# The first feed-forward layer of a fused two-block kernel as seven half-wide products in place of eight

## The chip, the cores and the metric

The kernel runs on one core of one Trainium2 chip, as one program. The metric is device time in microseconds (us) from launch to end. All data of the case is float32. The engines are called PE (TensorE), ACT (ScalarE), DVE (VectorE), POOL (GpSimd) and SP (SyncE, which only issues transfers here).

## What is computed

Two transformer-like blocks follow each other on 1024 tokens of width 1024. The change touches the feed-forward part of the first block:

```
h = rms_norm(x, g_pre_mlp[i])
f = jnp.square(jax.nn.relu(h @ w_up[i])) @ w_down[i]
x = x + rms_norm(f, g_post_mlp[i])
```

`w_up` is 1024 x 4096 and `w_down` 4096 x 1024. What is ahead of it (attention, convolution, a gated mix and the projection `w_o`) and what is behind it (a gate, and the whole second block) computes the same before and after the change.

## The kernel before, in words

Everything lies transposed: features on the 128 partitions, tokens along a row. The 1024 tokens are done in two halves of 512 (`HALF`), called `h` 0 and 1. A float32 product is made of three passes in a shorter float type: each operand is split into a high part (a cast on ACT) and a low part (the rest, a subtraction on DVE), and PE adds high x high, high x low and low x high (`three_passes`). One output tile of 128 features x 512 tokens over 1024 input features is thus 8 x 3 = 24 matmuls of 512 columns.

The stage of interest is written by `stream_phase`. A list `plan` holds its tiles in order, as (stage, half, index in the stage, kind, number), and each engine has a loop over `plan` of its own; the order within the engines' loops is written by hand, and semaphores tie them together. The stages `mix` and `wo` (the mix and the projection `w_o`) come first, then `mlp` for half 0 and for half 1. One `mlp` has four parts of 16 tiles: 8 tiles of kind `up` (a part of the first layer), then 8 of kind `down` (the second layer over these 8 x 128 hidden features, added into `f`). Weights arrive in blocks of 1 MB (`SLOT` = 2048 numbers in a partition), two output tiles in one, in a ring of three slots; SP issues the load of a block when the block three before it has been used. `Pieces` splits each half block: `split_ahead` makes its high part on ACT, and `lower_ahead` its low part on DVE, in place, up to four tiles ahead.

Of an `up` tile, ACT reads the result from PSUM with Relu, squares it and casts it (three instructions of 512 columns); DVE makes the low part, and a `down` tile waits for these. Of a `down` tile, ACT copies or DVE adds the result into `f`.

The norms between the stages need a sum over features: ACT squares tiles, DVE adds them up, PE multiplies the sum by ones (L1084), ACT takes the root (L1180), DVE the reciprocal (L1202). `residual_at` says at which tile of the plan DVE adds the normed `f` to the residual stream, `normed_at` where it writes the normed input of the next stage, `sum_at` where the root is taken. Before the change, half 1's residuals and its normed input lie in the `up` and `down` tiles 1 to 8 and 10 to 17 of `mlp` 0, half 0's own input in the tiles `wo` 3 to 6 of half 1. POOL has nothing to do in this stage.

Of the kernel before, what the change touches and what calls it, by code (L numbers as in the profile page):

```python
# [22 lines left out]
P = 128  # L23
# [126 lines left out]

def build(nc, io):
# [81 lines left out]
class Tiles:  # L233


    def __init__(self, k, name, readers, banks=4, first=0, spare=()):
        self.k, self.readers, self.banks, self.first, self.spare = k, readers, banks, first, spare
        self.moved = {}
# [12 lines left out]
    def may_fill(self, pe, n):  # L251
        back = self.banks + (len(self.spare) if n < 2 * self.banks + len(self.spare) else 0)
# [19 lines left out]
class Pieces:  # L272
# [6 lines left out]
    def __init__(self, k, filled, of_tile, places=4):  # L279

        self.k, self.base, self.filled, self.places, self.turned = k, len(k.piece_used), filled, places, 0
        self.what, self.last = [], {}
        index = {}
# [28 lines left out]
    def may_split(self, p, n, limit):  # L312
# [3 lines left out]
        if p - self.places >= self.base and self.last[p - self.places] >= n:  # L316
            return False
# [3 lines left out]
    def split_ahead(self, eng, n, limit=4, most=1000):  # L321

        while self.next - self.base < most and self.may_split(self.next, n, limit):
            p = self.next
            if p >= 4:
                eng.wait_ge(*self.k.piece_used[p - self.places])
# [51 lines left out]
def input_phase(k):  # L378
# [76 lines left out]
    k.rstd_sems = ((const_ready, 2), (conv_done, 4))  # L455
    k.branch_ready, k.gates_in = sem("branches_split"), [sem(f"gates_in{i}") for i in range(5)]
# [413 lines left out]
def stream_phase(k):  # L870
# [20 lines left out]
    acc2 = k.data(20480, HALF)  # L891

    def cols(h):
# [20 lines left out]
    sum_at = [("mix", 1, 2), ("wo", 1, 3), ("mlp", 0, 1), ("mlp", 0, 10), ("mlp", 1, 1), ("mlp", 1, 10), ("gate", 0, 0),  # L914
              ("gate", 0, 3), ("gate", 1, 3), ("in2", 0, 4)]
    sum_of = {place: acc2 if n in (2, 7) else acc for n, place in enumerate(sum_at)}
    moved_sum = {("gate", 0, 0): pps[2][:3], ("gate", 1, 3): ("gate", 1, 4), ("in2", 0, 4): ("in2", 0, 5)}
    sum_after = {moved_sum.get(place, place): place for place in sum_at}
    summed = [("mix", 1, 0), ("wo", 1, 2), ("mlp", 0, 0), ("mlp", 0, 9), ("mlp", 1, 0), ("mlp", 1, 9), ("gate", 0, 0),
# [4 lines left out]
    normed_at = {("wo", 1, 3): (0, "g_pre_mlp", (0, 1)), ("wo", 1, 4): (0, "g_pre_mlp", (2, 3)),  # L924
                 ("wo", 1, 5): (0, "g_pre_mlp", (4, 5)), ("wo", 1, 6): (0, "g_pre_mlp", (6, 7)),
# [8 lines left out]
    for t in range(KT):  # L934
        residual_at["mlp", 0, t + 1] = (1, "g_post_mix", (t,))
        normed_at["mlp", 0, t + 10] = (1, "g_pre_mlp", (t,))
        residual_at["mlp", 1, t + 1] = (0, "g_post_mlp", (t,))
# [2372 lines left out]
```

## Time and profile before

| | before |
|---|---|
| median of 3 runs | 2664.92 us (2663.51 to 2665.99) |
| profiled execution: its span, from the first instruction to the last | 2662.9 us |
| PE busy | 2604.2 us, 98% of the span |
| DVE, ACT, POOL busy | 54%, 40%, 15% |
| the two `mlp` halves, some 772.9 to 1489 us | PE without idle time, granted clock 1.00 |

The profiled execution has no time of its own beside its span; the median lies 2.0 us above the span, which is what lies around the instructions. The busy share of PE counts each matmul until its modelled end and so overlaps; a rate is read from how many matmuls start in a stretch, or from the distance of two rows.

### The profile page before, as it was taken

The numbers are of one execution on the slowest core, as the hardware profiler recorded it, in microseconds if no ns is written. First come the engines' busy times: TensorE is split into PE (matmuls) and PEld (weight loads), VectorE is DVE, ScalarE is ACT, GpSimd is POOL, SyncE is SP. The second block draws the span as 40 slices with busy tenths as digits, with TensorE's granted clock in tenths as the row PEclk, the third lists the DMA queues.
The fourth block names the chain that finished last, engine by engine and source line by source line (L and its number), as shares of the span: only waits on it lengthen the run. The fifth ranks groups of instructions, "written<-read, shape, count | busy, mean of one in ns | idle before, by whom it ended". The sixth has DMA issues, their size and how long they took to land.

```text
span 2662.9 us, 43735 instructions
## 1 busy us (share of the span) xinstructions
PE 2604.2 (98%) x18144; PEld 2059.4 (77%) x18144; DVE 1441.9 (54%) x2302; ACT 1058.0 (40%) x1940; POOL 395.5 (15%) x349
## 2 busy tenths in 40 slices
PE   8999999999999999999999999999999999999998
PEld 6887777778778888888888777866776677787876
DVE  8764443335776333464333576355667656655754
ACT  3242233323354432354234444334544545344521
POOL 3211111100000000000000000021112100456654
PEclk9999999999999999999999999999999999999999
DMA  5110011234322222222223222631111242100032
GB/s 181 64 48 33 32 56 64 68 131 167 149 84 93 94 95 95 95 95 95 95 95 111 79 86 89 258 140 50 46 48 45 88 186 83 61 19 19 19 127 95
DMA packets 46244, 238.36 MB, mean 90 GB/s; under 512 B 4448, under 2 KB 4576, under 8 KB 24672
## 3 DMA queue, kind: packets, MB, share of 16 engines
q1 hardware_dynamic: 38128, 209.35, 22.0%
q10 hardware_dynamic: 7920, 26.22, 2.5%
q8 instruction: 145, 2.38, 0.4%
q14 instruction: 51, 0.42, 0.0%
HBM read 205.40 MB, written 30.15 MB: 88 GB/s over the span
## 4 chain that ended last, share of the span: by engine, by line
PE 84%; DVE 8%; ACT 4%; issue 3%; DMA 1%; POOL 1%; DVEq 0%; ACTq 0%; SPq 0%; POOLq 0%
PE ps L373 58%; PE ps L2717 4%; PE ps L1592 2%; PE ps L1638 2%; PE ps L1618 2%; PE ps L1519 2%; PE ps L527 2%; PE ps L553 1%; PE ps L1521 1%; PE ps L1520 1%; PE ps L542 1%; ACT parts L329 1%; PE ps L1654 1%; DVE parts L352 1%; PE ps L2460 1%
## 5 line engine op out<-in xcount | busy, mean ns | idle before, releaser
L373 PE MATMUL ps<-parts,parts 128*128 128x512 f32 (+2 forms) x7896 | 1801.1, 388 | 15.7 <-DVE parts L722 9.5
L373 PEld LDWEIGHTS ps<-parts,parts 128*128 128x128 f32 x7896 | 1442.0, 188 | 364.7 <-issue 37.3
L352 DVE TENSOR_TENSOR parts<-ring,parts 128x1024 fp32r<-128x1024 f32 x240 | 295.9, 1236 | 221.0 <-ACT parts L329 213.7
L329 ACT CAST parts<-ring 128x1024 fp32r<-128x1024 f32 x243 | 252.8, 1044 | 193.7 <-PE ps L373 142.1
L352 POOL TENSOR_TENSOR parts<-ring,parts 128x1024 fp32r<-128x1024 f32 x62 | 152.1, 2455 | 455.4 <-DVE parts L329 455.4
L1999 POOL TENSOR_TENSOR phase_data<-phase_data,stream 128x512 f32<-128x512 f32 x12 | 18.4, 1538 | 1218.4 <-PE ps L1529 1218.4
L785 DVE TENSOR_TENSOR_SCAN stream<-stream 128x513 f32<-128x513 f32 (+3 forms) x96 | 94.0, 979 | 175.4 <-ACT stream L655 175.2
L1218 DVE TENSOR_TENSOR parts<-phase_data,parts 128x512 fp32r<-128x512 f32 (+1 forms) x110 | 76.9, 701 | 188.0 <-ACT parts L1147 170.0
L1717 ACT ACTIVATE stream<-stream,phase_data 128x640 f32<-128x640 f32 (+7 forms) x128 | 93.5, 731 | 84.0 <-DVE phase_data L1923 83.5
L1285 DVE TENSOR_TENSOR phase_data<-phase_data,ps 128x512 f32<-128x512 f32 x48 | 33.0, 687 | 118.8 <-PE ps L373 118.8
L1144 ACT ACTIVATE phase_data<-ps 128x512 f32<-128x512 f32 x64 | 38.3, 598 | 144.6 <-PE ps L373 144.2
L2926 ACT COPY phase_data<-ps 128x128 f32<-128x128 f32 x160 | 40.1, 266 | 110.1 <-PE ps L2717 104.3
L1519 PE MATMUL ps<-parts,parts 128*128 128x512 f32 x168 | 76.1, 453 | 4.0 <-DVE parts L352 2.1
L1618 PE MATMUL ps<-constants,stream 128*128 128x128 f32 x528 | 76.3, 278 | 3.2 <-ACT stream L1717 2.4
L1923 DVE CUSTOM_DVE_ANT_0 stream<-ps,phase_scratch 128x640 f32<-128x640 f32 (+4 forms) x96 | 54.4, 598 | 46.0 <-PE ps L1592 44.4
L2485 POOL TENSOR_TENSOR stream<-normed,phase_scratch 128x256 f32<-128x256 f32 x90 | 65.6, 762 | 92.3 <-ACT normed L2479 92.3
L1592 PE MATMUL ps<-phase_data 64*128 64x512 f32 (+3 forms) x384 | 74.4, 491 | 4.0 <-DVE phase_data L1923 4.0
L1618 PEld LDWEIGHTS ps<-constants,stream 128*128 128x128 f32 x528 | 59.2, 141 | 24.6 <-issue 9.9
L1638 PE MATMUL ps<-stream,phase_data 128*64 128x128 f32 x1056 | 76.6, 281 | 0.2 <-ACT stream L1726 0.2
L1726 ACT COPY stream<-ps 128x512 f32<-128x512 f32 (+1 forms) x85 | 43.9, 516 | 71.5 <-PE ps L1618 59.4
L3064 DVE TENSOR_TENSOR stream<-stream,ps 128x128 f32<-128x128 f32 x128 | 36.6, 286 | 62.9 <-PE ps L2717 52.9
L1638 PEld LDWEIGHTS ps<-stream,phase_data 128*64 128x64 f32 x1056 | 55.9, 136 | 15.7 <-issue 14.0
(344 smaller groups left out, 3038.9 us busy)
## 6 DMA issues: line engine op xcount, KB each, us to landing
ring<-in_weights SPq DMA_DIRECT2D x158, 1024.0 KB, 4.9
raw_keep<-phase_scratch SPq DMA_DIRECT2D x21, 256.0 KB, 2.3
normed<-gates_keep ACTq DMA_DIRECT2D x1, 4096.0 KB, 13.6
stream<-in_xT ACTq DMA_DIRECT2D x2, 2048.0 KB, 8.9
h_keep<-parts SPq DMA_DIRECT2D x1, 4096.0 KB, 15.6
x_keep<-stream ACTq DMA_DIRECT2D x1, 4096.0 KB, 17.3
parts<-h_keep SPq DMA_DIRECT2D x1, 4096.0 KB, 14.0
out_T<-stream SPq DMA_DIRECT2D x16, 256.0 KB, 2.1
```

What stands on the lines that cost most here:

```text
L329: cast(self.hi(p), self.whole(p)).then_inc(self.k.hi_ready, 1)
L352: g.tensor_tensor(self.lo(p), self.whole(p), self.hi(p).bitcast(F32), ALU.subtract).then_inc(self.k.lo_ready, 1)
L373: last = pe.matmul(out, a, b, start=i == 0 and a is ah and b is bh, stop=i == len(pairs) - 1 and a is al)
L785: step(v.tensor_tensor_scan(back, back, back, 1.0, ALU.mult, ALU.min))
L1218: return v.tensor_tensor(lo, whole_, hi.bitcast(F32), ALU.subtract)
L1519: pe.matmul(in3_bank, hi, H[:, t], start=t == 0, stop=False)
L1592: last = pe.matmul(k.ps[:, to:to + w * P], qr[rows(g), j, t * P:(t + 1) * P], keys[:, (first + c) * P:(first + c + w) * P], start=True, st ...
L1618: last = pe.transpose(out[:, 2 * x + g], ss[:, 2 * (pair_no[i] % 2) + g, at:at + P], ident)
L1638: last = pe.matmul(k.bank(unit_bank[unit])[rows(g), j * P:(j + 1) * P], vsvw[:, 0 if kind == "sel" else 1, first + kt, rows(g)], pts[:, pl ...
L1717: a.activation(tile, tile, ACT.Exp, bias=neg_max[:, n:n + 1], scale=-1.0, accum_out=sums[:, n:n + 1]).then_inc(e_ready, 1)
L2485: g.tensor_tensor(b.off[:, c % 2, l], b.mab(c), over_pairs(b.level[:, l]), ALU.mult).then_inc(k.off_ready, 1)
L2717: last = pe.matmul(out[rows(e), m], lhs(2 * i + m, e), rhs(2 * i + m, e), start=True, stop=True)
```

## The change

The first layer is done by one level of Strassen's method (in Winograd's form). Two `up` tiles that share a weight block form a "quad" `g`: 256 hidden features x 512 tokens, from 1024 x 256 weights. Weights and input are cut in 2 x 2 blocks (input features in two halves of 512; the 256 features in two tiles; the 512 tokens in two halves of 256). Where the eight block products were 48 matmuls of 512 columns, seven products of 4 x 3 = 12 matmuls of 256 columns take their place, 84 in all. In PE's order they are, with the bank that each adds into: B11 (x), B21 (y), T2 (x), and in the second tile's place T3 (z), T1 (x), T4 (z), B22 (x). T1 to T4 are sums of the input blocks. Between them ACT copies the bank x or z to SBUF (`copy_quad`, four times), and DVE adds banks into these copies (`add_quad`, three times); PE waits for the copy or the addition before it goes on in the same bank. Relu and square are now one instruction on DVE (`square_ff`).

The sums of weight blocks are made on POOL, four subtractions or additions of 512 columns for a quad (`sum_weights`), and of the input blocks also on POOL, four of 256 columns for each of four `i` in a half (`sum_inputs`). ACT then casts 1024, 1024, 1024 and 512 columns for a quad (`cast_weights`), and DVE makes as many low parts (`lower_weights`), each of which waits until all four sums of its quad are there. The sums of quad g lie where those of quad g-2 lay, so POOL waits for the end of quad g-2.

The normed input of `mlp` is written at `quad_at`: `wo` 3 to 6 for half 0, two tiles each; for half 1 it moves to tiles 56 to 59 of `mlp` 0. `quad_split_at` splits it one tile later. Residuals of `mlp` move from the tiles 1 to 8 to the tiles 8 to 11, two at a time, and half 0's `g_ple` input to the tiles 56 to 60. `down` tiles take three PSUM banks in turn in place of four, and add their inputs in the order 1, 0, 3, 2, ...

```diff
+    quad_at = {("wo", 1, 3 + i): (0, i) for i in range(4)} | {("mlp", 0, 56 + i): (1, i) for i in range(4)}
+    quad_split_at = {("wo", 1, 4 + i): (0, i) for i in range(4)} | {("mlp", 0, 57 + i): (1, i) for i in range(4)}
...
-        residual_at["mlp", 0, t + 1] = (1, "g_post_mix", (t,))
-        normed_at["mlp", 0, t + 10] = (1, "g_pre_mlp", (t,))
...
+        residual_at["mlp", 0, 8 + i] = (1, "g_post_mix", (2 * i, 2 * i + 1))
+        residual_at["mlp", 1, 8 + i] = (0, "g_post_mlp", (2 * i, 2 * i + 1))
...
+            for t in range(4):
...
+                pe.matmul(out, hi, x_hi, start=first and t == 0, stop=False, skip_group_check=True)
+                pe.matmul(out, hi, x_lo, start=False, stop=False, skip_group_check=True)
+                last = pe.matmul(out, lo, x_hi, start=False, stop=t == 3, skip_group_check=True)
...
+        def quad_second(g):
...
+            if g:
+                pe.wait_ge(*quad_added.at(3 * g))
+            product(g, "z", (1, 1), "T3", True).then_inc(quad_mm.sem, 1)
+            pe.wait_ge(*quad_copied.at(4 * g + 2))
+            product(g, "x", (2, 0), "T1").then_inc(quad_mm.sem, 1)
+            pe.wait_ge(*quad_copied.at(4 * g + 3))
+            product(g, "z", (2, 1), "T4").then_inc(quad_mm.sem, 1)
+            pe.wait_ge(*quad_added.at(3 * g + 2))
+            product(g, "x", (3, 0), "B22").then_inc(tiles.filled, 1)
...
+        def sum_weights(g):
...
+            if g:
+                g_.wait_ge(tiles.filled, wo_1_read if g == 1 else quad_tile(g - 2, 1) + 1)
+            else:
+                g_.wait_ge(tiles.filled, mix_1_read)
+            block_landed(k, g_, quad_slot(g))
...
+            g_.tensor_tensor(two[:, 1], w11, w21, ALU.subtract).then_inc(weight_sums.sem, 1)
+            g_.tensor_tensor(w21, w21, w22, ALU.add).then_inc(weight_sums.sem, 1)
+            g_.wait_ge(*weight_sums.at(4 * g + 2))
+            g_.tensor_tensor(two[:, 0], w21, w11, ALU.subtract).then_inc(weight_sums.sem, 1)
+            g_.wait_ge(*weight_sums.at(4 * g + 3))
+            g_.tensor_tensor(four[:, 0], w12, two[:, 0], ALU.subtract).then_inc(weight_sums.sem, 1)
...
+        sum_weights(0)
+        for h in range(2):
+            for i in range(4):
+                sum_inputs(h, i)
+            for g in range(QUADS * h + 1 - h, QUADS * h + QUADS):
+                sum_weights(g)
...
+        def lower_weights(g, i):
...
+            v.wait_ge(*weight_sums.at(4 * g + 4))
+            v.wait_ge(*weight_hi.at(4 * g + i + 1))
...
+            add_quad(g, quarter(m, 1), "x", 5 * g + 4, 4 * g + 3)
+            if inside:
+                lower_weights(g + 1, 1)
+            add_quad(g, quarter(m, 0), "z", 5 * g + 5, 4 * g + 2)
+            square_ff(h, m)
+            if inside:
+                lower_weights(g + 1, 2)
+            else:
+                pieces.lower_ahead(v, n)
+            square_ff(h, m - 1)
+            lower_ff(h, m)
+            if inside:
+                lower_weights(g + 1, 3)
+            else:
+                lower_ff(h, m - 1)
```

Where the change moves instructions, first DVE in the tiles `wo` 3 and 4 of half 1, before. L1202 is the reciprocal, L352 the low part of a weight piece, L1263 the normed input, L1218 its low part, L1214 the addition of a square.

```order
L1202 RECIPROCAL phase_scratch<-phase_scratch 128x512
L352 TENSOR_TENSOR parts_1024_153<-ring,parts_1024_138 128x1024
L1263 SCALAR_TENSOR_TENSOR normed<-stream,constants,phase_scratch 128x512 x2
L1218 TENSOR_TENSOR parts_8192_56<-normed,parts_8192_56 128x512 x2
L1214 TENSOR_TENSOR phase_data<-phase_data,phase_scratch 128x512
```

The same place of the changed kernel, up to the second pair (L375 is the low part of a piece, L1616 the normed input, L1493 its low part, L1489 the addition of a square):

```order
L1477 RECIPROCAL phase_scratch<-phase_scratch 128x512
L375 TENSOR_TENSOR parts_1024_155<-ring,parts_1024_140 128x1024
L1616 SCALAR_TENSOR_TENSOR normed<-stream,constants,phase_scratch 128x512 x2
L1489 TENSOR_TENSOR phase_data<-phase_data,phase_scratch 128x512
L375 TENSOR_TENSOR parts_1024_158<-ring,parts_1024_144 128x1024
L1493 TENSOR_TENSOR parts_8192_56<-normed,parts_8192_56 128x512 x2
L1493 TENSOR_TENSOR parts_2048_67<-phase_data,parts_2048_66 128x2x256
L1616 SCALAR_TENSOR_TENSOR normed<-stream,constants,phase_scratch 128x512 x2
```

A pair's three low parts now stand ahead of the next pair's normed input, and the first of them waits for the four POOL sums of its pair. POOL's queue at the start of the stage is this in the changed kernel (L1257 to L1262 `sum_weights(0)`, L1272 to L1277 `sum_inputs(0, 0)`; three more of these follow):

```order
L1257 TENSOR_TENSOR phase_data<-ring 128x512
L1258 TENSOR_TENSOR ring<-ring 128x512
L1260 TENSOR_TENSOR phase_data<-ring 128x512
L1262 TENSOR_TENSOR phase_data<-ring,phase_data 128x512
L1272 TENSOR_TENSOR phase_data<-normed 128x256
L1274 TENSOR_TENSOR normed<-normed 128x256
L1275 TENSOR_TENSOR phase_data<-normed,phase_data 128x256
L1277 TENSOR_TENSOR phase_data<-normed,phase_data 128x256
```

Before, POOL has no row here at all. The sums of the weights stand ahead of those of the input. Last, DVE over one quad inside a part (quad 1 of half 0) in the changed kernel, where L1521 is `add_quad`, L1493 the low part of a hidden tile, L1505 `lower_weights` of quad 2 and L1529 `square_ff`:

```order
L1521 TENSOR_TENSOR phase_data<-ps,phase_data 128x256
L1493 TENSOR_TENSOR parts_8192_65<-phase_data,parts_8192_65 128x512
L1505 TENSOR_TENSOR parts_1024_155<-ring,parts_1024_148 128x1024
L1521 TENSOR_TENSOR phase_data<-ps,phase_data 128x256
L1505 TENSOR_TENSOR parts_1024_6756<-phase_data,parts_1024_152 128x1024
L1521 TENSOR_TENSOR phase_data<-ps,phase_data 128x256
L1529 SCALAR_TENSOR_TENSOR phase_data<-phase_data 128x512
L1505 TENSOR_TENSOR parts_1024_158<-ring,parts_1024_140 128x1024
L1529 SCALAR_TENSOR_TENSOR phase_data<-phase_data 128x512
L1493 TENSOR_TENSOR parts_8192_65<-phase_data,parts_8192_65 128x512
L1505 TENSOR_TENSOR parts_512_6757<-phase_data,parts_1024_144 128x512
```

Before, DVE had for the same two tiles two rows of L352 (128x1024) and two of L1218 (128x512). The second addition of three (which B22 of the same quad waits for) now stands behind the first `lower_weights` of the next quad.

## Rows read from the trace of the kernel before

**Rows 1.** The page's head and its first section.
```profile
span 2662.9 us, 43735 instructions
...
PE 2604.2 (98%) x18144; PEld 2059.4 (77%) x18144; DVE 1441.9 (54%) x2302; ACT 1058.0 (40%) x1940; POOL 395.5 (15%) x349
```

**Rows 2.** Timeline of PE, 700 to 1640 us (start, us, what, count).
```profile
750.65 33.95 PE L373 MATMUL ps<-parts,parts 128*128 128x512 f32 x144
...
835.83 306.61 PE L373 MATMUL ps<-parts,parts 128*128 128x512 f32 x1320
```

**Rows 3.** Waits, 784.4 to 1142.3 us (who waited for whom: us, times, longest).
```profile
DVE parts L1218 <- ACT parts L1147: 85.7, 26, 5.2
ACT phase_data L1144 <- PE ps L373: 72.9, 28, 4.5
```

**Rows 4.** Timeline of ACT, 98 to 128 us: copies of 256-column tiles.
```profile
116.82 0.37 ACT L631 COPY phase_data<-ps 128x256 f32<-128x256 f32 x1 [0.93 <-PE ps L373]
...
122.47 0.37 ACT L631 COPY phase_data<-ps 128x256 f32<-128x256 f32 x1 [1.93 <-PE ps L373]
```

**Rows 5.** Groups by shape, 784.4 to 1142.3 us.
```profile
L352 DVE TENSOR_TENSOR parts<-ring,parts 128x1024 fp32r<-128x1024 f32 x64 | 78.4, 1226 | 44.4 <-ACT parts L329 44.4
L329 ACT CAST parts<-ring 128x1024 fp32r<-128x1024 f32 x64 | 66.7, 1043 | 68.6 <-PE ps L373 68.6
L1218 DVE TENSOR_TENSOR parts<-phase_data,parts 128x512 fp32r<-128x512 f32 x40 | 27.7, 692 | 91.2 <-ACT parts L1147 85.7 <-ACT parts L1110 5.5
```

**Rows 6.** Groups of the whole run: 256 columns from PSUM, and POOL's.
```profile
L3037 DVE TENSOR_TENSOR phase_data<-phase_data,ps 128x256 f32<-128x256 f32 x15 | 6.2, 415 | 0.0
...
L2451 POOL TENSOR_TENSOR normed<-phase_data,normed 128x256 f32<-128x256 f32 x15 | 10.9, 728 | 0.0
```

**Rows 7.** Timeline of POOL, 2401 to 2405 us: a chain.
```profile
2401.95 1.26 POOL L3118 TENSOR_TENSOR phase_data<-phase_data 128x512 f32<-128x512 f32 x1
2403.32 1.56 POOL L3120 TENSOR_SCALAR phase_data<-phase_data,constants 128x512 f32<-128x512 f32 x1
```

**Rows 8.** Timeline, 1729.5 to 1736 us: DVE beside POOL.
```profile
1729.91 3.52 POOL L1999 TENSOR_TENSOR phase_data<-phase_data,stream 128x512 f32<-128x512 f32 x2 [1189.71 <-PE ps L1529]
...
1730.47 1.80 DVE L352 TENSOR_TENSOR parts<-ring,parts 128x1024 fp32r<-128x1024 f32 x1 [4.96 <-ACT parts L329]
...
1734.19 1.29 POOL L1999 TENSOR_TENSOR phase_data<-phase_data,stream 128x512 f32<-128x512 f32 x1 [0.77 <-PE ps L1529]
```

**Rows 9.** Timeline, 66 to 71 us: DVE beside POOL.
```profile
67.32 2.41 POOL L352 TENSOR_TENSOR parts<-ring,parts 128x1024 fp32r<-128x1024 f32 x1 [2.46 <-DVE parts L329]
67.75 2.52 DVE L712 SCALAR_TENSOR_TENSOR phase_data<-stream,constants,phase_scratch 128x512 f32<-128x512 f32 x1
```

**Rows 10.** Timelines of DVE and of SP, 745 to 776 us.
```profile
752.09 3.35 DVE L1202 RECIPROCAL phase_scratch<-phase_scratch 128x512 f32<-128x512 f32 x1 [5.79 <-ACT phase_scratch L1180]
755.48 1.23 DVE L352 TENSOR_TENSOR parts<-ring,parts 128x1024 fp32r<-128x1024 f32 x1
756.62 1.41 DVE L1263 SCALAR_TENSOR_TENSOR normed<-stream,constants,phase_scratch 128x512 f32<-128x512 f32 x2
...
750.39 23.44 SPq L225 DMA_DIRECT2D ring<-in_weights  x3
```

**Rows 11.** The ring's loads on SP's queue, 700 to 900 us.
```profile
DMA to landing us min/median/max: 4.7/4.8/4.9
```

**Rows 12.** PE after a wait: timeline 1636 to 1650 us, and windows (us, busy, granted clock, DMA share, GB/s).
```profile
1643.91 2.07 PE L1084 MATMUL ps<-phase_scratch,constants 128*128 128x512 f32 x2 [4.28 <-DVEq L1239]
1644.99 5.24 PE L373 MATMUL ps<-parts,parts 128*128 128x512 f32 x13
...
1636.00:1644.00 8.00, 3.72 (x17) 0.86 0.39 132
1644.00:1652.00 8.00, 8.00 (x24) 0.72 0.01 2
```

More of the change, by code:

```diff
@@ L282, in __init__ @@
         self.what, self.last = [], {}
+        self.not_before, self.after = {}, {}
         index = {}
@@ L993, in stream_phase, with quad_slot, quad_tile @@
             k.used[one] = (tiles.filled, n + 1)
+    quad_mm, quad_copied, quad_added, weight_sums, weight_hi, weight_lo, input_sums, input_ready, ff_square = k.spent
+    def quad_slot(g):
+        return START["mlp", g // QUADS] + 8 * (g % QUADS // 4) + g % 4
+    def quad_tile(g, odd):
+        return at["mlp", g // QUADS, "up", 2 * (g % QUADS) + odd]
+    for h in range(2):
+        for c in range(FF_PARTS):
+            g = QUADS * h + 4 * c + 3
+            first = pieces.of_tile[at["mlp", h, "down", 8 * c]][0]
+            assert (first + pieces.turned) % 4 == 0
+            now = quad_tile(g, 1)
+            for i, (after, n) in enumerate(((quad_mm.at(5 * g + 2), now), (quad_mm.at(5 * g + 3), now + 1),
+                                            (quad_mm.at(5 * g + 5), now + 1), ((tiles.filled, now + 1), now + 1))):
+                pieces.after[first + i], pieces.not_before[first + i] = after, n
@@ L994, in stream_phase @@
+    up_read = [at["mlp", h, "up", 31] + 1 for h in range(2)]
     pp_hi, pp_lo = k.data_part(16384, 2, SLOT // 2), k.data_part(18432, 2, SLOT // 2)
@@ L1037, in _ @@
         sums = 0
         for n, (st, h, i, s, m) in enumerate(plan):
+            if s == "up":
+                (quad_second if m % 2 else quad_first)(QUADS * h + m // 2)
+            if s == "up" and (st, h, i) in sum_after:
+                sums += 1
+                pe.wait_ge(ss_ready, sums)
+                pe.wait_ge(root_done, sums - 1)
+                pe.matmul(k.bank(4), k.const("ones"), sum_of[sum_after[st, h, i]], start=True,
+                          stop=True).then_inc(ss_done, 1)
@@ L1114, in _ @@
             tile = tiles.bank(n)
-            pieces.split_ahead(a, n)
+            if s == "up":
+                quad(n, h, m)
+            else:
+                pieces.split_ahead(a, n)
+            if here in quad_at:
+                state.normed += 2
+            if here in quad_split_at:
+                cast_inputs(*quad_split_at[here])
+            if here == ("mlp", 0, 61):
+                cast_fourth(1)
+            if (st, h) == ("wo", 1) and m >= 6:
+                cast_weights(0, m - 6)
+            if s == "down" and m % 8 >= 6 and (h, m // 8) != (1, 3):
+                cast_weights(QUADS * h + m // 8 * 4 + 4, m % 8 - 6)
             if here == ("wo", 0, 0):
@@ L1141, in _ @@
                 mix_cast[h, m] = k.act.inc(a.copy(mix_hi[h][:, m], mix[:, m]))
-            elif s == "up":
-                x = ff_whole[:, KT + m % 8]
-                tiles.read(a.activation(x, tile, ACT.Relu), n)
-                a.wait_ge(tiles.emptied["a"], tiles.rank[n])
-                step(a.activation(x, x, ACT.Square))
-                ff_hi[h, m] = k.act.inc(a.copy(ff[:, m % 8], x))
             elif s == "pp":
```

271 lines of the change are left out of this document (245 added, 26 removed).

## The prediction, made before the changed kernel ran

> **What bounds the kernel now.** I read the page first: PE is busy for 98% of the span, the other engines for 54% at most [rows 1]. The timeline of PE shows for the stage in question that there is nothing between: 1320 matmuls of 512 columns in 306.61 us, which is 0.2323 us each and 5.575 us for a tile of 24 [rows 2]. The waits of this stretch have no row of PE; ACT and DVE wait for PE (L1144) or for each other (L1218) [rows 3]. So the feed-forward stage goes by PE's columns alone, and fewer of them are worth their full time, as long as the other engines, which get new work, stay ahead.
>
> **What the change removes on PE.** 64 `up` tiles of 5.575 us are 356.8 us. In their place stand 32 quads of 7 products of 12 matmuls, 2688 of 256 columns. That form is in the trace: two tiles of 24 such matmuls each end 5.65 us apart (ACT copies each as it ends) [rows 4], so 0.1177 us each, 1.413 us a product, 9.89 us a quad, 316.5 us in all. PE's part of the sum is -40.3 us. Though the weights are loaded afresh for half as many columns, the cost is 0.507 of a 512-column matmul. By the Trainium skill, page "TensorE: Matmul & The Clock Gate", section "Back-to-back issue gap" (columns over 2.4 GHz and 2.5 ns), it would be 109.2 against 215.8 ns, 293.5 against 331.5 us, a gain of 38.0; the trace is slower than the rule in both forms.
>
> **What POOL and DVE then do to each other.** A POOL instruction of 512 columns takes 1.26 us alone, the next that depends on it starts 1.37 after it [rows 7]; four are 5.3 us. Beside DVE it is different. A DVE instruction with two inputs in SBUF that began under one of POOL took 1.80 us in place of 1.23 [rows 5, 8], another 2.52 [rows 9] in place of 0.70 [rows 10]; and two POOL instructions with that DVE one between took 3.52, where twice 1.29 is 2.58 [rows 8]. They take turns: a POOL and a DVE instruction of 1024 columns together need 3.52 - 1.29 = 2.23 us. Of this DVE's own step is 1.14 (755.48 to 756.62) [rows 10], and 1.09 is POOL's. The same rule is on the skill's page "SBUF — State Buffer", section "Who interferes with whom": the pair of ports is locked for a whole instruction, and the loser blocks fully. The trace agrees. All of DVE's work of a quad is of that kind but the additions from PSUM (0.42 us, 256 columns [rows 6]). Each step is some 0.09 less than the time shown, since the next starts ahead of its end: 1.14 for 1024 columns, 0.60 for a low part of 512, 0.66 for Relu and square [rows 5, 10].
>
> POOL may sum quad g+1 from the end of quad g-1. In a part of four quads this puts sums into the second and the third quad; those for the first two fit beside the `down` tiles before. Walk from the first quad, from its start. T4 ends at 6 x 1.413 and 0.2 after, 8.65. ACT casts until 9.8 (1.04 [rows 5]), DVE's third `lower_weights` ends at 11.1. From here until the second quad's addition for B22, DVE has to do: Relu and square 0.66, two low parts 1.2, one more 0.6, the first `lower_weights` of the next quad 1.14 (which waits for all four sums), the addition 0.42; POOL's turns are 4 x 1.09 = 4.36. That is 8.4, so 19.5 (the addition of y reads PSUM and hides under a POOL turn). PE wants B22 at 9.89 + 8.48 = 18.4: **1.15 us lost**. The second quad ends at 2 x 9.89 + 1.15 = 20.9. In the third DVE is late from the start. From 19.5 on it has 1.14 (`lower_weights`), 0.33 (addition), 0.66, 1.14, 0.66 and 3 x 0.60 of low parts, 5.7 (the addition of y hides under a POOL turn); POOL has 4.36; then 1.14 and 0.42 for the addition that B22 waits for. That is 31.1; PE wants B22 at 20.9 + 8.48 = 29.4: with the hand-overs **1.8 lost**. Without turns both would be nothing. The fourth has no sums beside it and catches up. At its end the first piece for `down` is lowered behind an addition and Relu and square: 8.65 + 0.1 + 0.42 + 0.75 + 1.23 = 11.1, PE wants it at 9.9: **1.2 lost**. Together 4.15 us a part, eight parts: **+33**. Bounds: from below no turns, 8 x 1.2 = 10; from above, each turn costs an instruction in full (1.29 for 1.09, and 0.1 for each hand-over), some 2 us more a part, 49.
>
> **Start of half 0.** Today the input of `mlp` is normed at `wo` 3 to 6 and in time. PE reaches `mlp` four tiles after 750.65, at 773.0 [rows 2]. In the change POOL first sums the weights of quad 0. Their block is asked for at 750.39 and lands 4.8 later, 755.2 [rows 10, 11]; four sums, with DVE's piece and two norms of 755.5 to 758 between, end near 761.5. Then rounds that can't overlap, since DVE's low parts of pair i stand ahead of pair i+1: norm two tiles 1.4 [rows 10], four POOL sums of 256 columns 3.0 (0.73 each and hand-overs [rows 6]), three low parts 2.0 [rows 5], 6.5 with the waits. The first pair's sums end at 764.7, and three rounds more are 784.2; its low parts 1.9 and `lower_weights(0, 0)` 1.2 later, at 787.3, PE may start: a wait of 14.3 us. Two `add_square` and piece rows take turns with POOL in it, some 1.2: **+15.5**. Nothing covers it, as `w_o` is done and every product needs all four input tiles; the wo tiles behind which it could hide end at 773. Nothing is late behind it: the weights of the following quads lie ready. After a wait of 4.28 us the granted clock was 0.72 over the 8 us that follow it, against 1.00 [rows 12]: 4.5 us at the lower of the two levels (1.2 GHz), half of it lost, **+2.3**. Bounds: 6 (rounds of 4.5 us, as if POOL ran beside DVE) to 22 (rounds of 8).
>
> **Small terms.** The second root of each half now comes at `down` tile 6: root 0.7, reciprocal 3.35 [rows 10], `lower_weights` 1.23 and the ones matmul against 5.6 us of tile 7, about 1 us late, a further one with a table load: +1 for each half, **+2**. Half 1's input beside the last `down` tiles of half 0 makes DVE some 7.5 us a tile for three tiles against 5.6, three PSUM banks and the two easier tiles behind absorb it: +1 (0 to 3). Residuals in `down` tiles 8 to 11 are 3 us of DVE more a tile in 5.6 with 1.2 of pieces: 0. Copies on ACT: each has one product (1.41) against 0.4, 0. A wait of ACT for the third sum (`cast_weights`, 1) stands ahead of nothing that PE needs sooner. Loads: each has one part's rhythm as before, and no more bytes: 0. The gate stage finds its input five tiles ahead: 0.
>
> **Sum.** -40.3 + 33 + 15.5 + 2.3 + 2 + 1 = +13.5 us. The profiled span is 2662.9 and the median of the runs 2.0 above; I take the median, 2664.9, and get 2678.4, **2678 us**.
>
> **Rivals.** (1) *The turns cost nothing*, because POOL's instructions fall where DVE waits for ACT or PE: parts at 10 in place of 33, the rest as above, 2655 us. For it: DVE is half idle before [rows 1]. Against it: the lengthened instructions [rows 8, 9], and that DVE has 8.5 us of work in a quad of 9.9. From stalls of under 2.4 us a part on, the change gains. 0.22. In 0.03 of it the start is covered too and all of the gain shows, 2627. (2) *Half the turns* or short rounds at the start: 2666, 0.12. (3) *Hand-overs between products cost PE*: each of 224 products begins with waits for a copy or addition; at 0.1 us each it is +22 and 2700. For it: a late chain through ACT (the cast of a hidden tile waits for DVE and stands ahead of the copy which T1 needs). Against it: the 256-column tiles hand over without a gap [rows 4]. 0.14, with everything else that makes it over 2692. (4) Forecast: turns and start as worked out, 2667 to 2692: 0.52.
>
> **Range and chances.** The forecast's own range is 2667 to 2692. To leave out no more than 2 in 10 it goes down to rival 1 and close to rival 3: 2653 to 2697. A measurement of this kernel tells 0.2%, 5.3 us, from no change. Below 2659.6: rival 1 and a third of rival 2, 0.26. Within: 0.08. Above 2670.2: 0.66.
>
> **What the profile of the changed kernel would show.** PE: 2688 matmuls of 256 columns, near 45 in 5 us where nothing waits. A wait of PE of 10 to 20 us near 773 us, ended by DVE's `lower_weights`, and the clock below 1.00 behind it. Waits of 1 to 2 us for `add_quad` in the second and third quad of each part and none of size in the first; one of 1.2 for the first piece of `down`. POOL's 512-column sums at some 1.9 to 2.4 us where DVE works and at 1.27 in `down`; DVE's rows lengthened likewise. If POOL's and DVE's means stay at 1.27 and 1.23, or the wait near 773 is under 5 us, I am wrong and the time is lower; if PE waits on ACT's copies in every quad, it is higher.

## The result, and the profile after

| | before | changed |
|---|---|---|
| median | 2665.45 us (2663.51 to 2666.16) | 2705.86 us (2705.35 to 2707.2) |
| ratio | | 1.0156 [1.0141, 1.017] |
| span of the profiled execution | 2662.9 us | 2703.7 us |

The changed kernel is 40.4 us slower. I had said 2678 us, 13.5 us slower, with a range from 2653 to 2697: the direction was right, the size was not. The page of the changed kernel, its head and first section, beside [rows 1]:

```profile
span 2703.7 us, 47034 instructions
...
PE 2582.6 (96%) x19296; PEld 2095.6 (78%) x19296; DVE 1674.5 (62%) x2536; ACT 1076.3 (40%) x2014; POOL 637.3 (24%) x509
```

PE has 22 us less to do and the span is 41 longer. Windows show where. First the second part of half 0, cut where PE's quads and its `down` tiles begin (bounds; length, then busy us and instructions of PE, weight loads, DVE, ACT and POOL; granted clock; DMA share; GB/s):

```profile
892.64:902.53 9.89, 9.89 (x85) 9.89 (x84) 6.51 (x10) 6.13 (x9) 0.00 (x0) 1.00 0.35 114
902.53:913.57 11.04, 10.16 (x87) 9.95 (x85) 11.01 (x11) 6.06 (x10) 7.04 (x4) 1.00 0.35 129
913.57:925.52 11.95, 10.44 (x87) 10.03 (x86) 11.91 (x12) 5.89 (x10) 7.01 (x4) 1.00 0.22 77
925.52:935.41 9.89, 9.89 (x86) 9.84 (x84) 6.09 (x11) 4.10 (x8) 0.00 (x0) 1.00 0.21 84
935.41:981.18 45.77, 44.76 (x195) 36.15 (x193) 20.62 (x20) 11.70 (x13) 11.08 (x8) 1.00 0.25 91
```

The second and third quad have POOL in them, DVE is busy to the end of each, and they take 11.04 and 11.95 us in place of 9.89. That much was forecast. The `down` tiles of this part take 45.77; eight tiles of 5.575 are 44.6, and the 1.2 between is the forecast wait for the first piece. Three other places lost time: the first quad of half 0, which runs in part at the low clock (forecast, 2.3 us), its first `down` tiles (1 us was forecast) and its last (1 us):

```profile
793.77:806.16 12.39, 12.39 (x85) 12.39 (x85) 8.66 (x12) 5.63 (x8) 0.00 (x0) 0.78 0.04 7
...
839.03:892.64 53.61, 48.35 (x199) 37.53 (x197) 42.08 (x38) 19.81 (x29) 13.46 (x8) 0.97 0.21 78
...
1113.67:1164.86 51.19, 45.04 (x192) 35.88 (x193) 41.17 (x46) 20.70 (x30) 28.54 (x24) 1.00 0.26 97
```

The waits of PE in the changed kernel (who for whom: us, times, longest) say what ended them there:

```profile
PE ps L1150 <- issue: 25.7, 2, 20.7
PE ps L1242 <- DVEq L1580: 14.4, 3, 5.1
PE ps L1150 <- DVE phase_data L1521: 13.7, 16, 0.9
...
PE ps L1150 <- ACT phase_data L1326: 5.4, 8, 0.7
```

20.7 us is the wait ahead of half 0's first product. The other of the 25.7 is the start of half 1, 5.0. L1242 is the sum of squares for a root, which waits for DVE's signal at L1580, 5.1 us in the first `down` part and 5.0 in half 1's (the third, 4.3, stands behind the stage, in the kernel before too [rows 12]). The third row is the second and third quads, and the fourth a copy on ACT that PE waits for once in each third quad. In 839 to 893 the timeline of DVE (start, us, what) has this round three times, once with POOL beside it:

```profile
857.65 0.75 DVE L1590 SCALAR_TENSOR_TENSOR phase_scratch<-phase_data,constants,phase_scratch 128x512 f32<-128x512 f32 x1
858.44 0.69 DVE L1595 TENSOR_TENSOR stream<-stream,phase_scratch 128x512 f32<-128x512 f32 x1
860.83 1.23 DVE L375 TENSOR_TENSOR parts<-ring,parts 128x1024 fp32r<-128x1024 f32 x1 [1.70 <-ACT parts L352]
...
868.07 1.99 DVE L375 TENSOR_TENSOR parts<-ring,parts 128x1024 fp32r<-128x1024 f32 x1 [1.71 <-ACT parts L352]
869.98 3.49 DVE L1489 TENSOR_TENSOR phase_scratch<-phase_scratch 128x512 f32<-128x512 f32 x2
873.39 1.78 DVE L1590 SCALAR_TENSOR_TENSOR phase_scratch<-phase_data,constants,phase_scratch 128x512 f32<-128x512 f32 x1
```

Two things lengthen a round. POOL's sums for the next part (from 867.67) stretch 1.23 to 1.99, a pair of 1.48 to 3.49 and 0.75 to 1.78, and a round from 6.4 or 7.2 us to 11.0. And in each round DVE waits 1.7 us for ACT's cast of a weight piece (L352), which stands on ACT behind the squares of the residuals that DVE has only just written. The experiments take these apart.

### The profile page after: what moved, and what is told of

The parts are those of the page before. It is cut to its first block, busy times and chain, and to the rows that moved or that the text cites. A ratio compares the mean times of both kernels' runs of the same rounds, so it can differ in the third digit from the quotient of the medians.

```text
span 2703.7 us, 47034 instructions
## 1 busy us (share of the span) xinstructions
PE 2582.6 (96%) x19296; PEld 2095.6 (78%) x19296; DVE 1674.5 (62%) x2536; ACT 1076.3 (40%) x2014; POOL 637.3 (24%) x509
## 4 chain that ended last, share of the span: by engine, by line
PE 71%; DVE 15%; issue 6%; ACT 5%; POOL 2%; DMA 1%; DVEq 0%; ACTq 0%; SPq 0%; POOLq 0%
PE ps L396 40%; PE ps L3077 4%; PE ps L1952 2%; PE ps L1998 2%; PE ps L1150 2%; DVE parts L1493 2%; PE ps L1978 2%; PE ps L1151 2%; PE ps L1152 2%; PE ps L1879 2%; PE ps L552 2%; ACT parts L352 1%; PE ps L578 1%; PE ps L1881 1%; DVE parts L375 1%
## 5 line engine op out<-in xcount | busy, mean ns | idle before, releaser
L396 PE MATMUL ps<-parts,parts 128*128 128x512 f32 (+2 forms) x6360 | 1449.6, 388 | 22.8 <-DVE parts L747 8.8
L396 PEld LDWEIGHTS ps<-parts,parts 128*128 128x128 f32 x6360 | 1155.4, 189 | 307.3 <-issue 45.0
L375 DVE TENSOR_TENSOR parts<-ring,parts 128x1024 fp32r<-128x1024 f32 x176 | 220.3, 1263 | 171.6 <-ACT parts L352 162.9
L1150 PE MATMUL ps<-parts,parts 128*128 128x256 f32 x896 | 255.5, 285 | 44.8 <-issue 25.7
L375 POOL TENSOR_TENSOR parts<-ring,parts 128x1024 fp32r<-128x1024 f32 x62 | 152.4, 2460 | 454.8 <-DVE parts L352 454.8
L1151 PE MATMUL ps<-parts,parts 128*128 128x256 f32 x896 | 253.3, 283 | 0.0
L1152 PE MATMUL ps<-parts,parts 128*128 128x256 f32 x896 | 253.1, 283 | 0.0
L352 ACT CAST parts<-ring 128x1024 fp32r<-128x1024 f32 x179 | 184.4, 1043 | 114.8 <-PE ps L396 61.1
L1150 PEld LDWEIGHTS ps<-parts,parts 128*128 128x128 f32 x896 | 171.0, 191 | 50.8 <-issue 26.5
L1257 POOL TENSOR_TENSOR phase_data<-ring 128x512 f32<-128x512 f32 x32 | 50.0, 1564 | 636.6 <-DMA ring<-in_weights 504.7
L1151 PEld LDWEIGHTS ps<-parts,parts 128*128 128x128 f32 x896 | 170.2, 190 | 0.3
L1152 PEld LDWEIGHTS ps<-parts,parts 128*128 128x128 f32 x896 | 170.2, 190 | 0.0
L1493 DVE TENSOR_TENSOR parts<-phase_data,parts 128x512 fp32r<-128x512 f32 (+1 forms) x112 | 105.8, 946 | 16.4 <-ACT parts L1422 11.0
L1326 ACT COPY phase_data<-ps 128x256 f32<-128x256 f32 x128 | 46.7, 371 | 120.4 <-PE ps L1152 120.4
L1505 DVE TENSOR_TENSOR parts<-ring,parts 128x1024 fp32r<-128x1024 f32 x64 | 91.5, 1430 | 4.8 <-ACT parts L1321 4.0
## 6 DMA issues: line engine op xcount, KB each, us to landing
normed<-gates_keep ACTq DMA_DIRECT2D x1, 4096.0 KB, 13.6
```

Of the source, the lines that this page charges most:

```text
L352: cast(self.hi(p), self.whole(p)).then_inc(self.k.hi_ready, 1)
L375: g.tensor_tensor(self.lo(p), self.whole(p), self.hi(p).bitcast(F32), ALU.subtract).then_inc(self.k.lo_ready, 1)
L396: last = pe.matmul(out, a, b, start=i == 0 and a is ah and b is bh, stop=i == len(pairs) - 1 and a is al)
L1150: pe.matmul(out, hi, x_hi, start=first and t == 0, stop=False, skip_group_check=True)
L1151: pe.matmul(out, hi, x_lo, start=False, stop=False, skip_group_check=True)
L1152: last = pe.matmul(out, lo, x_hi, start=False, stop=t == 3, skip_group_check=True)
```

## The experiments

Fourteen kernels ran, each with its own profile. This table has what PE's first matmuls of each quad and part give in us (a dash: as in the changed kernel, to 0.3); r4_before_moved, which has no quads, is told below. The second and third quads are those of the later parts of a half; where DVE makes the sums of quad 1 too (r6, r7, r9, r10, r11 and r13), the second quad of a half's first part took 10.0 to 11.4 us. The last column counts from the end of the fourth quad, 9.89 us after its start, and so holds the 1.2 us ahead of the first `down` matmul beside the 51.19 above.

| kernel | median | ratio to before | wait ahead of half 0, first quad | 2nd, 3rd quad | first `down` parts (h 0, 1) | last `down` part of h 0 |
|---|---|---|---|---|---|---|
| changed | 2705.9 | 1.0156 | 20.7, 12.4 | 11.04, 11.95 | 53.6, 54.5 | 52.4 |
| r1_root_late | 2695.2 | 1.0114 | -, - | - | 47.8, 47.8 | - |
| r2_small_sums | 2654.6 | 0.9961 | 17.6, 11.6 | 9.89, 9.89 | 46.9, 46.9 | 46.5 |
| r3_norm_first | 2702.9 | 1.0142 | 17.7, 12.0 | - | 55.0, 53.5 | - |
| r5_dve_sums | 2683.0 | 1.0070 | -, 11.6 | 9.89, 10.29 | 54.2, 54.9 | - |
| r6_joined | 2681.8 | 1.0065 | 13.4, 13.9 | 9.89, 10.29 | 47.5, 47.6 | 69.8 |
| r7_joined_inputs | 2664.3 | 0.9998 | 9.6, 13.9 | 9.89, 10.29 | 49.1, 47.4 | 53.8 |
| r8_small_in_first_down | 2689.7 | 1.0097 | -, - | - | 46.9, 46.8 | - |
| r9_spread | 2664.7 | 1.0001 | 9.6, 13.9 | 9.89, 10.30 | 47.4, 47.5 | 52.8 |
| r10_spread_start | 2661.9 | 0.9988 | 8.8, 13.9 | 9.89, 10.30 | 47.4, 47.5 | 52.7 |
| r11_late_pieces | 2668.6 | 1.0016 | 8.8, 13.9 | 9.89, 10.30 | 51.1, 51.9 | 52.2 |
| r12_after_late_pieces | 2700.9 | 1.0135 | -, 11.6 | - | 52.0, 52.0 | - |
| r13_deferred | 2651.7 | 0.9950 | 8.8, 13.9 | 9.89, 10.29 | 45.4, 45.4 | 47.5 |
| r14_after_deferred | 2691.3 | 1.0101 | -, 11.6 | - | 47.5, 46.9 | - |

**Are the turns with POOL the loss?** r2_small_sums. Its edit, for every quad but the first:

```diff
+            if g:
...
+                g_.tensor_tensor(w21[:, 0:8], w21[:, 0:8], w22[:, 0:8], ALU.add).then_inc(weight_sums.sem, 1)
...
+                g_.tensor_tensor(four[:, 0], w12, w11, ALU.subtract).then_inc(weight_sums.sem, 1)
+                return
```

> The changed kernel with three of the four weight sums on POOL cut from 512 to 8 columns for every quad but the first; the fourth sum stays whole but takes w12 - w11, and the second weight pair is read from the block in place of its sum. So it leaves out most of the weight sums; every instruction, wait and load stays, and ACT, DVE and PE do the same amount of work. Theory A (POOL and DVE take turns): quads 2 and 3 of each part come near 9.9 us (from 11.04 and 11.94), POOL's and DVE's mean times fall, the first down part becomes 1 to 2 us shorter, in all 21 to 26 us less: 2680 to 2685. Theory B (DVE has too much to do in a quad by itself, or waits for ACT): the two quads stay over 11 us and the time stays within 5 us of 2706.

Measured 2654.6 us, ratio 0.9961 [0.9947, 0.9975]: 51 us less, twice what theory A gave; the quads themselves came as it said. Its third quad of the second part, to be read against 913.57 above, and the first `down` tiles:

```profile
898.55:908.44 9.89, 9.89 (x86) 9.89 (x85) 8.40 (x12) 6.10 (x10) 3.83 (x4) 1.00 0.30 106
...
831.82:878.69 46.87, 46.70 (x198) 36.57 (x197) 36.03 (x38) 19.92 (x29) 5.02 (x8) 1.00 0.25 89
```

DVE's same 12 instructions are 8.40 us busy in place of 11.91. By place, 50 of the 51 are 25.6 in the second and third quads (8 x 3.2), 14.4 in the two first `down` parts, 5.9 in the last of half 0, 3.0 in the start and 1.2 in the first quads. So half of what POOL's weight sums cost lies outside these quads; the prediction had put nearly all of it inside.

**Is it the place of POOL's work beside the first `down` tiles?** r8_small_in_first_down makes the same sums small, but only for the quads 4, 5, 20 and 21.

> The changed kernel with three of the four POOL sums cut to 8 columns for the quads 4, 5, 20 and 21 alone (most of the weight sums of these four quads is left out, and one weight pair is read from the block). They are the sums that POOL makes beside the first down tiles of either half, where the residuals and the second root stand. Theory A (the first down part takes 53.6 and 54.5 us because POOL's turns make DVE late in front of the root): 47 us in either, time 2690 to 2694. Theory B (residuals and root cost this by themselves in the changed kernel, since DVE has more in a down tile, whatever POOL does): the two parts stay over 52 us and the time at 2703 or more.

Measured 2689.65, 1.0097 [1.0082, 1.0112]. Theory A: the two parts fell by 6.8 and 7.7 us, and no quad and no other part of the stage moved by more than 0.3. Of the 7, 5.1 us are PE's wait at L1242, which is gone, and the rest is the low clock behind it: in the changed kernel that window has a granted clock of 0.97 and 48.35 us of busy PE, in r2_small_sums 1.00 and 46.70.

**Or the root, or the moved residuals?**

```diff
-    sum_at = [("mix", 1, 2), ("wo", 1, 3), ("mlp", 0, 7), ("mlp", 0, 14), ("mlp", 1, 7), ("mlp", 1, 14), ("gate", 0, 0),
+    sum_at = [("mix", 1, 2), ("wo", 1, 3), ("mlp", 0, 7), ("mlp", 0, 30), ("mlp", 1, 7), ("mlp", 1, 30), ("gate", 0, 0),
...
-    summed = [("mix", 1, 0), ("wo", 1, 2), ("mlp", 0, 0), ("mlp", 0, 13), ("mlp", 1, 0), ("mlp", 1, 13), ("gate", 0, 0),
+    summed = [("mix", 1, 0), ("wo", 1, 2), ("mlp", 0, 0), ("mlp", 0, 29), ("mlp", 1, 0), ("mlp", 1, 29), ("gate", 0, 0),
```

> The changed kernel with one thing altered: the second root of each mlp half (sum of squares of the residual stream) is taken at tile 30 (a down tile of the second part) in place of tile 14, its result being needed only at tile 56. Nothing is left out. Theory A (the first down tiles lose their time because the root stands right behind the residuals: PE waits 5.1 us at 884.5 for the sum of squares, then runs some us at the lower clock): the first down part goes from 53.6 us to about 47 in either half, some 1 us comes back at tile 30, so the time is 2693 to 2696. Theory B (the residuals themselves make DVE too late for the down tiles, the wait only shows at the sum): the wait goes over to the copies of the down tiles and little is won, 2703 to 2706.

Measured 2695.16, 1.0114 [1.0099, 1.0129]: theory A, with 1.6 us given back in each second part. And the moves without the rest of the change:

> The kernel before with only the residuals of mlp moved to the tiles 8 to 11, two at a time, the roots to the tiles 7 and 14, and the norms behind them to the tiles 16 to 23 (the change moves residuals and roots to the same tiles; no seven products, no POOL). Nothing is left out. Theory A (residuals two to a tile and a root right behind them cost PE time by themselves): the first down part of each half takes 5 to 9 us more, 2675 to 2683. Theory B (they only cost beside the change's new work of DVE, ACT and POOL): 2665 to 2667.

Measured 2666.51, 1.0006 [0.9997, 1.0015]. Theory B, and within its interval also the 1 us a half that the prediction gave the second root. In 784 to 1142 us its PE is busy for 357.03 of 358.00 us, where the kernel before has 358.00.

**The hand-over between ACT and DVE.** First DVE's side: the low part of the piece behind the residuals.

```diff
-            late = st in ("mix", "wo") and n > 0
+            late = st in ("mix", "wo") and n > 0 or s == "down" and 8 <= i < 13
```

> The changed kernel with one thing altered: in the down tiles 8 to 12 DVE makes the low part of the weight piece behind the residuals in place of ahead of them. Nothing is left out. In the changed kernel's trace a round of two residuals takes 6.4 us without POOL beside it and 11.0 with it; 1.3 us of it DVE waits for the piece's cast, which stands on ACT behind the squares of the residuals before. Theory A (these hand-overs share in the 53.6 and 54.5 us of the first down part): 2 to 3 us less in either half, 2699 to 2702. Theory B (only POOL's turns matter there): 2704 to 2707.

Measured 2700.93, 1.0135 [1.012, 1.015]: theory A by its smaller end, 1.6 and 2.5 us. The number hides two changes. The wait of 5.1 us at L1242 is gone, as with the root's date or POOL's sums, and a new one stands in tile 9, since the piece now stands behind the reciprocal and the residuals of tile 8:

```profile
848.76 34.92 PE L396 MATMUL ps<-parts,parts 128*128 128x512 f32 x144 [3.65 <-DVE parts L375]
```

Then ACT's side, the squares of a tile behind the next tile's cast:

```diff
                 pieces.split_ahead(a, n)
+            for x in late_squares:
+                square(*x)
+            late_squares = []
...
+            late_squares = [x for x in squares_at[here] if x[3]]
```

> The changed kernel with that one alteration on ACT (squares behind the next piece's cast in the down tiles of mlp). Nothing is left out. Theory A: the first down parts go from 53.6 and 54.5 to 49 to 51 us (rounds of 6.4 us come to about 5.1, those with POOL's four turns from 11.0 to 9.5), the last of half 0 from 52.4 to 50, time 2695 to 2699. Theory B: less than 2 us in each part, 2703 or more.

Measured 2691.25, 1.0101 [1.0087, 1.0114]. The first `down` parts came out better than theory A said, 47.5 and 46.9 us. The last of half 0 did not: it stayed at 52.3 where theory A had 50. The same place of DVE's timeline, now without a wait in the round (5.4 us a round), though POOL's turns still stand in the last:

```profile
861.20 0.69 DVE L1601 TENSOR_TENSOR stream<-stream,phase_scratch 128x512 f32<-128x512 f32 x1
861.81 1.22 DVE L375 TENSOR_TENSOR parts<-ring,parts 128x1024 fp32r<-128x1024 f32 x1
...
867.24 2.32 DVE L375 TENSOR_TENSOR parts<-ring,parts 128x1024 fp32r<-128x1024 f32 x1
869.49 3.48 DVE L1495 TENSOR_TENSOR phase_scratch<-phase_scratch 128x512 f32<-128x512 f32 x2
```

So three different changes (POOL's sums of two quads, the hand-over on ACT, the root's date) each take the same 6 to 8 us from a first `down` part. They are not parts of a sum: DVE was late for one deadline, the sum of squares at L1242, and any one of them nearly or wholly makes it. r13_deferred below has two of them, the root's date and the hand-over, and its parts take 45.4 us, 8 and 9 less and not 12 and 14.

**Can DVE do the sums itself?** r5_dve_sums puts four DVE instructions of 512 columns where POOL's stood.

> The changed kernel with the four weight sums of the third and fourth quad of each part made by DVE in the quad before (in the place ahead of its first low part of that quad) in place of POOL. Nothing is left out. DVE gets four instructions of 512 columns more in two quads of four, 2.4 us, and loses four turns with POOL of some 1.1 us. Theory A (a sum on POOL costs DVE more than one of its own): quads 2 and 3 come to 9.9 to 10.3 us from 11.04 and 11.94, 2681 to 2688. Theory B (DVE has no 2.4 us to give: adding 7.5 us of its own work it has 9.9 in a quad of 9.89, in an order of waits): the quads stay at 10.7 to 11.5 and the time is 2692 or more.

Measured 2682.97, 1.007 [1.0054, 1.0087], theory A. Its third quad:

```profile
909.30:919.59 10.29, 10.15 (x86) 9.95 (x85) 10.15 (x16) 6.30 (x10) 0.00 (x0) 1.00 0.31 109
```

16 instructions in 10.15 us, against 12 in 11.91 with POOL: for DVE, a sum that it makes is cheaper than one that POOL makes beside it.

**The start, and the parts together.** r3_norm_first moves the next pair's norm ahead of the low parts of the pair before.

> The changed kernel with one block of DVE's code moved up: in the tiles wo 4 to 6 of half 1 and mlp 57 to 59 the normed input of the next pair is written ahead of the low parts of the pair before. Nothing is left out. Theory A (the start of half 0 is a chain of rounds norm, four POOL sums, three low parts, which can't overlap in the written order): POOL goes on with the next pair at once, each of three rounds gets 2 to 3 us shorter, PE's wait at 793 falls from 20.7 to 12 to 15 us; half 1's start, 8 us over its plain time, gains 2 to 4; 2693 to 2698. Theory B (the chain is POOL's, its weight sums and sixteen input sums beside DVE): less than 2 us, 2704 to 2706.

Measured 2702.93, 1.0142 [1.0127, 1.0157]: the wait fell by 3.0 us, more than theory B's 2 and far less than theory A's 6 to 9, and half 1 won nothing. A round now takes 5.8 us in place of 6.7 in two of the three, and in these DVE has no idle time: POOL's sums stand beside its rows and lengthen them, a 512-column one from 0.68 to 1.21.

> The changed kernel with five alterations together, nothing left out: the sums of quads 1, 2, 3 of half 0's and half 1's first part and of quads 2, 3 of the other parts on DVE; the second root at tile 30; the next pair's norm ahead of the low parts; POOL's sums for quad 16 ahead of its input sums of half 1; the piece for the first down tile lowered ahead of Relu and square. Worked out from the runs so far: 2706 - 10.7 (root) - 2.9 (norm) - 20 to 25 (quads 2 and 3) - 7 (pieces, 1.18 in six parts) - 4 (turns at the start of half 0) - 4 (start of half 1): 2652 to 2658, below the kernel before. Theory B (these are all one shortage of DVE, so what is won in one place is asked for in the next): 2665 or more.

Measured 2681.84, 1.0065 [1.005, 1.008], 24 us over theory A's upper end. The time fits theory B's "2665 or more", its reason doesn't: the start, the root and the quads behind the second came as worked out, the pieces won 4.4 us of 7, the first two quads took 1.9 us more than in the changed kernel (DVE has quad 1's sums to make there), and the last `down` part of half 0 took 69.8 us. POOL's timeline:

```profile
1118.89 1.26 POOL L1261 TENSOR_TENSOR phase_data<-ring 128x512 f32<-128x512 f32 x1 [66.67 <-DMA ring<-in_weights]
...
1124.01 0.72 POOL L1276 TENSOR_TENSOR phase_data<-normed 128x256 f32<-128x256 f32 x1
```

I had put the weight sums of quad 16 ahead of half 1's input sums. Its block lands only at 1118.9 us, as a slot of the ring comes free late, and the input sums stood behind that wait in POOL's queue, DVE behind them and PE behind DVE.

> The kernel of r6_joined with the sixteen sums of input blocks of each half made by DVE too, right behind their pair's norm; POOL keeps only the weight sums of quad 0 and of the first two quads of a part. Nothing is left out. Theory A (the rounds at the start go by hand-overs between DVE and POOL; four sums of 256 columns are 1.4 us of DVE in place of 3.1 on POOL): the wait at the start of half 0 gets 5 to 9 us shorter than in r6_joined, half 1's last down tiles lose nothing, 2645 to 2652. Theory B (DVE alone has 6.5 us a tile at the start of half 1 and 5.6 to do it in): half 1 loses what half 0 wins, same time as r6_joined within 3 us.

Measured 2664.33, 0.9998 [0.9989, 1.0007]. The start won 3.8 us more and 16 us came back in the last `down` part, but half 1's input still cost 7.6 (53.8 against 46.2 in half 1's last part). That is neither theory: 12 us over A's upper end, and 17.5 better than B.

> The kernel of r7_joined_inputs with half 1's input spread over more of the last down tiles: norm and sums in the tiles 56, 58, 60, 61, low parts in 57, 59, 61, 62, the fourth sum's low part in 62 (from 56 to 59 and 57 to 61). Nothing is left out. Theory A (the last down part of half 0 takes 53.8 us because four tiles in a row ask DVE for more than a tile's 5.6 us; a round took 8.4 us in that run): the part goes to 46 to 48 us, time 2656 to 2660. Theory B (DVE's whole work in these eight tiles, some 42 us, is what doesn't fit): 51 us or more, 2661 or more.

Measured 2664.68, 1.0001 [0.9992, 1.0011]: theory B, 52.8 us.

> The kernel of r9_spread with two alterations at the start of half 0: the weight sums of quad 0 on DVE behind the third pair's sums (POOL now has nothing in that stretch), and the last pair's first low part and the first weight pair's ahead of its other low parts. Nothing is left out. Theory A (in r7_joined_inputs POOL's four sums took some 4.4 us of turns from DVE at 755 to 761, where four on DVE are 2.4, and 1.2 us of low parts can go behind PE's start): 3 to 4 us less than r9_spread. Theory B (POOL's work was free there, as ACT was waited for): 2 us more than r9_spread.

Measured 2661.91, 0.9988 [0.9979, 0.9998]: 2.8 us less, a little under theory A's 3 to 4. The two kernels' single runs overlap and their profiled spans differ by 1.3, so the direction is A's and the size is not sure. In its last `down` part DVE is busy for 42.88 of 52.66 us and waits in each round:

```profile
1100.76 0.68 DVE L1678 TENSOR_TENSOR phase_data<-phase_data,ps 128x512 f32<-128x512 f32 x1
1103.13 1.22 DVE L375 TENSOR_TENSOR parts<-ring,parts 128x1024 fp32r<-128x1024 f32 x1 [1.69 <-ACT parts L352]
```

> The kernel of r10_spread_start with DVE's low part of a weight piece put behind the residuals (down tiles 8 to 12) and behind the input's low parts (tiles 57 to 62 of half 0), in place of ahead of them. Nothing is left out. In the traces DVE waits there for ACT's cast of the piece, and ACT for DVE's residual or addition before it. Theory A (this ping-pong costs 1 to 2 us a tile while DVE is late): 2 to 6 us less than r10_spread_start. Theory B (DVE catches up in the tiles behind by itself, or the piece now comes too late for PE): no gain or a loss.

Measured 2668.55, 1.0016 [1.0006, 1.0025], theory B: the last part won 0.5 us, but in tile 8 the piece stood behind the reciprocal as well, as in r12_after_late_pieces, and PE waited 3.9 us for it, so the first `down` parts lost 4.

> The kernel of r10_spread_start with one thing altered on ACT: in the down tiles of mlp the squares of a tile (of residuals, and of the last down part) come behind the cast of the next tile's weight piece in place of ahead of it. Nothing is left out. Theory A (DVE and ACT wait for each other in every round: DVE's addition, ACT's square, ACT's cast, DVE's low part): a round gets 1.5 to 2 us shorter, the last down part of half 0 goes from 52.7 to 46 to 48 us, the first ones from 47.4 to 46.5, time 2654 to 2658. Theory B (DVE's plain work is what is too much): 51 us or more, 2660 to 2663.

Measured 2651.72, 0.995 [0.9937, 0.9964]. Theory A: the last part, at 47.5 us, is in its range, and the first parts (45.4 for 46.5) and the time (2 us under its lower end) are better. The same two rows of its timeline, and its last `down` part:

```profile
1102.29 0.68 DVE L1684 TENSOR_TENSOR phase_data<-phase_data,ps 128x512 f32<-128x512 f32 x1
1103.11 1.23 DVE L375 TENSOR_TENSOR parts<-ring,parts 128x1024 fp32r<-128x1024 f32 x1
```

```profile
1083.18:1130.68 47.50, 44.94 (x194) 35.98 (x193) 43.88 (x64) 22.02 (x32) 5.45 (x4) 1.00 0.25 95
```

DVE is busy for 43.88 of 47.50 us: the same 64 instructions, 5 us sooner. This kernel beats both others, the one before by 13.6 us. It still leaves 8.8 us of wait ahead of half 0 and 4.0 in its first quad.

## Why the prediction missed, step by step

- *PE's columns, -40.3*: right. A quad where nothing waits takes 9.89 us in every kernel, as said.
- *Turns in the second and third quad, 1.15 and 1.8 lost*: right, 1.15 and 2.06; they are 25.6 us in eight parts, 23.6 were given. The walk through the third quad had one wait, for the addition ahead of B22. The trace has two, and the other, 0.7 us, is for a copy on ACT.
- *The piece behind the addition, 1.2 lost*: right, 1.18, in six parts of eight. In the two others it lies in the gap that the ones matmul makes: 7 us, where 9.6 were given.
- *"Residuals in `down` tiles 8 to 11 are 3 us of DVE more a tile in 5.6 with 1.2 of pieces: 0"*, and *the second root, "+1 for each half"*: these failed, and the largest share of the miss is here, 12.4 of 27.5 us. The first `down` parts took 53.6 and 54.5 us. The profile of before has two ones matmuls there too, some 1 us each, and r2_small_sums has 46.9, so 7 us a half are new, 14.4 in place of 2. The sum of DVE's busy times did fit (42.08 us even with the turns in it, and eight tiles give 44.6). What I left out was that POOL's sums for the next part's two quads, which I had called free "beside the `down` tiles before", take turns with the residuals, and that a round also holds 1.7 us of waiting for ACT. r4_before_moved shows that the moves alone are as cheap as I had said; r8 and r14 show that it takes both: with either gone the part falls to about 47.
- *"Half 1's input +1"*: failed, 6.6 us in its last `down` part and 1.4 of low clock in the quad behind it. 5.9 of these go with POOL's weight sums for the quads 16 and 17 (r2_small_sums), which stand behind sixteen input sums in POOL's queue and so fall on DVE's last low parts.
- *Start of half 0, 15.5*: too small, 20.7. The rounds were right (6.72 us, 6.5 given) and began 1.4 late. The mis-sized term is "its low parts 1.9 and `lower_weights(0, 0)` 1.2 later". POOL goes on to quad 1's sums at once, and these four instructions of DVE took 7.3 us:

```profile
786.38 3.42 DVE L1493 TENSOR_TENSOR parts<-normed,parts 128x512 fp32r<-128x512 f32 x2 [2.90 <-POOL phase_data L1277]
789.73 1.75 DVE L1493 TENSOR_TENSOR parts<-phase_data,parts 128x512 fp32r<-128x512 f32 x1
791.39 2.28 DVE L1505 TENSOR_TENSOR parts<-ring,parts 128x1024 fp32r<-128x1024 f32 x1
```

- *The clock behind that wait, +2.3*: right, the first quad took 12.39 at a granted clock of 0.78, 2.5 us over.
- *"The gate stage finds its input five tiles ahead: 0"*: failed by 1.1 us. PE waits for DVE's last addition into `f` at the first tile behind the `mlp`, where the kernel before has no wait:

```profile
1530.42 1.89 PE L396 MATMUL ps<-parts,parts 128*128 128x512 f32 x7 [1.08 <-DVE phase_data L1647]
```

The terms as measured: -40.3 + 25.6 + 7 + 14.4 + 8.0 + 20.7 + 2.5 + 1.1 = +39.0 us; the span grew by 40.8, and 1.8 of it I haven't placed. Rival 1, turns that cost nothing, was priced at 2655 us; the kernel without most of them ran in 2654.6, so its condition didn't hold, and the price was near, in part by luck: the wait ahead of half 0 was 17.6 us there for 15.5, and the pieces 7 for 10. Rival 3 named the time (over 2692) for a reason that holds only in small part. The hand-overs between products cost nothing by themselves, since a first or fourth quad takes 9.89 us. Its "late chain through ACT" is there, 5.4 us in all, but only in the third quads, where POOL holds DVE up; in r5_dve_sums it is gone, and in r2_small_sums 0.5 us of it is left.

One rule, that POOL and DVE take turns when both have their operands in SBUF, was read from the trace in advance and then charged only in the quads and, with 1.2 us, at the start. POOL's queue had to be laid beside DVE's over the whole stage: into the `down` tiles, and behind the last input sum.

## What to carry to other kernels

When work goes to POOL, charge it to DVE wherever POOL's queue can put it beside DVE's work on SBUF operands, here some 1.1 us for each instruction of 512 columns (DVE's 11.91 us against 8.40 with three of them made small); if DVE needs less for the operation itself (0.6 us here), DVE should do it. A stretch in which an engine's busy time fits may still be late when each round passes through a second engine and back; put on that engine what the next round waits for ahead of what closes this one. And before an instruction is moved up in a queue, ask when its data lands: what is queued behind it will wait as long.

## What the hardware showed that I had not expected

The clock's loss didn't follow the length of the wait. Behind 20.7 us without a matmul the first quad took 12.39 us in the changed kernel and 11.60 in r5_dve_sums, r12_after_late_pieces and r14_after_deferred; behind 8.8 us in r13_deferred it took 13.92, granted clock 0.82 in that window:

```profile
781.68:795.60 13.92, 12.50 (x85) 12.29 (x86) 11.82 (x17) 5.63 (x8) 0.00 (x0) 0.82 0.13 38
```

PE is idle for 1.4 us of it, because DVE has quad 1's sums to make as well; the other 2.6 us over 9.89 are the low clock. So the low clock cost 1.7 to 2.5 us behind the long wait and 2.6 behind the short one: shortening the wait from 20.7 to 8.8 us gave back its length and nothing of what comes behind it.
